# A decoder trunk's feed-forward stages: seven half-size block products per tile in place of eight, with the weight differences made on GpSimd

## The reference, cut to what matters

```
def swiglu(h, wg, wu, wd):
    return (jax.nn.silu(h @ wg) * (h @ wu)) @ wd
...
h = rmsnorm(x, ffn_norm_g[layer, 0])
x = x + 0.5 * swiglu(h, ffn_w_gate[layer, 0], ffn_w_up[layer, 0], ffn_w_down[layer, 0])
```

## Time and profile before

| | |
|---|---|
| median of three runs | 2102.38 us |
| span of the profiled execution | 2100.5 us |
| TensorE matmuls, busy | 2081.9 us (99%) |
| VectorE busy | 1205.3 us (57%) |
| ScalarE busy | 732.8 us (35%) |
| GpSimd busy | 107.2 us (5%) |
| chain that ended last | almost all TensorE |

### The profile page before, as it was taken

How to read it: one execution, slowest core, us unless ns; L and a number is a source line. 1 busy time by engine, 2 the same in 40 slices (tenths; PEclk the granted TensorE clock), 3 DMA queues, 4 the chain that set the end, 5 groups by cost and what they waited for, 6 DMA issues and landing times.

```text
span 2100.5 us, 30045 instructions
## 1 busy us (share of the span) xinstructions
PE 2081.9 (99%) x11183; PEld 1693.5 (81%) x11183; DVE 1205.3 (57%) x1925; ACT 732.8 (35%) x1029; POOL 107.2 (5%) x143
## 2 busy tenths in 40 slices
PE   8999999999999999999999999999999999999998
PEld 6888888788888888888888888888866688888887
DVE  6435445595777896444346544435679855444345
ACT  4212223453445442222124222222467742222223
POOL 0000000001000000000010000000026500000000
PEclk9999999999999999999999999999999999999999
DMA  6333433332253324454453333332310123333321
GB/s 174 100 100 91 112 88 93 92 92 72 61 141 96 86 81 120 103 117 104 110 114 103 100 100 90 100 100 76 110 46 1 41 71 100 92 99 91 100 87 64
DMA packets 357990, 195.17 MB, mean 93 GB/s; under 512 B 14891, under 2 KB 349878, under 8 KB 357894
## 3 DMA queue, kind: packets, MB, share of 16 engines
q1 hardware_dynamic: 355270, 184.21, 30.8%
q0 software_dynamic: 2624, 9.67, 2.9%
HBM read 191.07 MB, written 2.79 MB: 92 GB/s over the span
## 4 chain that ended last, share of the span: by engine, by line
PE 67%; DVE 4%; POOL 2%; issue 1%; ACT 0%; DVEq 0%; ACTq 0%; POOLq 0%
PE ps L1659 18%; PE ps L1657 18%; PE ps L1658 18%; PE ps L2276 1%; PE ps L2247 1%; POOL index_scores L490 1%; PE ps L2226 1%; PE ps L1989 1%; PE ps L1676 1%; PE ps L1991 1%; PE ps L1990 1%; PE ps L1677 1%; PE ps L1678 1%; POOL sq L487 1%; DVE w_lo L904 1%
## 5 line engine op out<-in xcount | busy, mean ns | idle before, releaser
L509 ACT ACTIVATE w_hi<-w_raw 128x1024 fp32r<-128x1024 f32 x351 | 371.7, 1060 | 1011.9 <-PE ps L1659 954.6
L1657 PE MATMUL ps<-h_hi,w_hi 128*128 128x512 f32 x1552 | 605.4, 390 | 0.0
L1658 PE MATMUL ps<-h_lo,w_hi 128*128 128x512 f32 x1552 | 603.8, 389 | 0.0
L1659 PE MATMUL ps<-h_hi,w_lo 128*128 128x512 f32 x1552 | 603.8, 389 | 0.0
L904 DVE TENSOR_TENSOR w_lo<-w_raw,w_hi 128x1024 fp32r<-128x1024 f32 x351 | 429.7, 1225 | 281.4 <-ACT w_hi L509 281.1
L1657 PEld LDWEIGHTS ps<-h_hi,w_hi 128*128 128x128 f32 x1552 | 291.4, 188 | 61.8 <-issue 1.7
L1659 PEld LDWEIGHTS ps<-h_hi,w_lo 128*128 128x128 f32 x1552 | 291.4, 188 | 60.6
L1658 PEld LDWEIGHTS ps<-h_lo,w_hi 128*128 128x128 f32 x1552 | 291.4, 188 | 60.0
L1657 PE MATMUL ps<-act_hi,w_hi 128*128 128x512 f32 x692 | 269.3, 389 | 0.0
L1659 PE MATMUL ps<-act_hi,w_lo 128*128 128x512 f32 x692 | 269.2, 389 | 0.0
L1658 PE MATMUL ps<-act_lo,w_hi 128*128 128x512 f32 x692 | 269.2, 389 | 0.0
(11 more groups left out here) (354 smaller groups left out, 2207.1 us busy)
## 6 DMA issues: line engine op xcount, KB each, us to landing
w_raw<-in_ffn_w_gate SPq DMA_DIRECT2D x88, 512.0 KB, 3.8
w_raw<-in_ffn_w_up SPq DMA_DIRECT2D x88, 512.0 KB, 3.8
w_raw<-in_ffn_w_down SPq DMA_DIRECT2D x64, 512.0 KB, 4.1
w_raw<-in_hy_w_in SPq DMA_DIRECT2D x44, 512.0 KB, 3.8
w_raw<-in_ffn_w_down SPq DMA_DIRECT2D x32, 384.0 KB, 3.5
w_raw<-in_hy_w_out SPq DMA_DIRECT2D x16, 512.0 KB, 3.8
acum_rows<-acum_scratch POOLq DMA_DIRECT2D x4, 1024.0 KB, 10.7
bias_rows<-line_scratch POOLq DMA_DIRECT2D x8, 512.0 KB, 6.8
```

The costliest lines, as they stand in the source:

```text
L509: act.activation(w_hi[:, s, :], w_raw[:, s, :], ACT.Copy).then_inc(hi_ready, 1)
L1657: pe.matmul(ps[:, bank, :], wh, rh[:, k, :], start=k == 0, stop=False)
L1658: pe.matmul(ps[:, bank, :], wh, rl[:, k, :], start=False, stop=False)
L1659: mm = pe.matmul(ps[:, bank, :], wl, rh[:, k, :], start=False, stop=k == nk - 1)
```

## The change

- The hidden tiles 4 to 21 of each stage (18 of 22; the first four stay as they were, `PLAIN`) are computed as a 2 x 2 block product with seven products instead of eight (`seven`). The 2 x 2 blocks of the weights are gate and up by the lower and upper half of the contraction; those of the input are the halves of the contraction by the halves of the tokens. Each product is 4 blocks x 3 matmuls of 256 columns, so a tile is 84 matmuls of 256 columns where it was 48 of 512.
- The products need sums and differences. Four blocks of the input are made once per stage by VectorE (`h_sums`, on `s_raw`, which ScalarE fills with eight scaled copies of `x`) and split into high and low parts (`s_high`, `s_low`). Per tile GpSimd makes four differences of weights of 128 x 512 (`weight_sums`): three into `mix_raw`, of which there is one, and one in place in the raw up unit. ScalarE rounds the 128 x 1536 of `mix_raw` (`t_high`), VectorE makes the low part (`t_low`). GpSimd starts a tile only when `t_low` of the tile before is done, and `load` now waits for its differences as well.
- The partial results are summed in PSUM where it can be done, and by small copies on ScalarE (`keep`, four of 128 x 256 per tile) and additions on VectorE (`gate_low`, `up_sums`, `gate_high`). TensorE waits for those copies between products (`kept`). The rounding of the activation moves from VectorE (L1042) to ScalarE (`act_high`).
- The down projection runs in phases of 4, 4, 4, 4 and 6 tiles. For the first four, two output columns are computed after each tile (`down_pack`: 24 matmuls of 512 columns), from one 512 KB unit that holds both. The last six tiles are done as eight down units at the stage's end.
- The loops over units are written out. The parameter transposes of `ffn0` come after its fourth tile. The bias rows of the attention are fetched after the last product of `ffn2` rather than during `ffn1`. Several semaphores are merged.

The core of the diff (of the two loops over `f` that follow `weight_sums`, the first is ScalarE's and the second VectorE's; `seven` and the last loop are TensorE's):

```
-PHASES = ((0, 8), (8, 8), (16, 6))
+HC = UC // 2
+PHASES = ((0, 4), (4, 4), (8, 4), (12, 4), (16, 6))
+PLAIN = 4
+BB, BA, BC = 0, 2, 6
...
+            def weight_sums(st, f):
+                u, k = gate_unit(st, f), (FT - PLAIN) * FFNS.index(st) + f - PLAIN
+                gate, up = w_raw[:, u % SLOTS, :], w_raw[:, (u + 1) % SLOTS, :]
+                pool.wait_ge(raw_landed[u % SLOTS], LAND[u])
+                pool.wait_ge(raw_landed[(u + 1) % SLOTS], LAND[u + 1])
+                if f > PLAIN:
+                    pool.wait_ge(t_lo_ready, k)
+                pool.tensor_tensor(mix_raw[:, 0:HC], up[:, 0:HC], gate[:, 0:HC], ALU.subtract).then_inc(t_made, 1)
+                pool.tensor_tensor(up[:, 0:HC], up[:, HC:UC], up[:, 0:HC], ALU.subtract).then_inc(t_made, 1)
+                pool.wait_ge(t_made, 4 * k + 1)
+                pool.tensor_tensor(mix_raw[:, HC:2 * HC], up[:, HC:UC], mix_raw[:, 0:HC], ALU.subtract).then_inc(t_made, 1)
+                pool.wait_ge(t_made, 4 * k + 3)
+                pool.tensor_tensor(mix_raw[:, 2 * HC:3 * HC], gate[:, HC:UC], mix_raw[:, HC:2 * HC], ALU.subtract).then_inc(t_made, 1)
...
+                for f in range(PLAIN, FT):
+                    nxt_unit = gate_unit(st, f) + 2
+                    if f == PLAIN:
+                        silu(f - 1)
+                    else:
+                        silu_half(f - 1, 1)
+                    if f == PLAIN:
+                        s_high(3)
+                    produce_hi(nxt_unit)
+                    act_high(f - 1)
+                    if f < FT - 1:
+                        t_high(f + 1)
+                    keep(f, 0)
+                    produce_hi(nxt_unit + 1)
...
+                for f in range(PLAIN, FT):
+                    nxt_unit = gate_unit(st, f) + 2
+                    added = 4 <= f - 1 < LAST + 4
+                    if f == PLAIN:
+                        scaled(f - 1)
+                    else:
+                        gate_high(f - 1)
+                    product(f - 1)
+                    if f == PLAIN:
+                        s_low(3)
+                    act_low(f - 1)
+                    if added:
+                        add_down(f - 1, 0)
+                    produce_lo(nxt_unit)
+                    if added:
+                        add_down(f - 1, 1)
+                    gate_low(f)
+                    produce_lo(nxt_unit + 1)
+                    if f < FT - 1:
+                        t_low(f + 1)
+                    if f < LAST + 4:
+                        produce_lo(nxt_unit + 2)
+                    up_sums(f)
...
+                def seven(f):
...
+                    product(b, gate, 0, *a11, True).then_inc(prod_done, 1)
...
+                    product(a, gate, HC, *a12, True).then_inc(unit_used, 1)
+                    pe.wait_ge(t_lo_ready, k + 1)
+                    pe.wait_ge(kept, 4 * k + 1)
...
+                    product(b, mixed, HC, *s2, False).then_inc(prod_done, 1)
...
+                    product(c, mixed, 0, *s1, True).then_inc(prod_done, 1)
+                    pe.wait_ge(lo_ready, u + 2)
+                    pe.wait_ge(kept, 4 * k + 2)
+                    product(b, up, 0, *s3, False).then_inc(prod_done, 1)
+                    pe.wait_ge(kept, 4 * k + 3)
...
+                    product(c, up, HC, *s4, False).then_inc(unit_used, 1)
+                    pe.wait_ge(kept, 4 * k + 4)
+                    product(b, mixed, 2 * HC, *a22, False).then_inc(prod_done, 1)
...
+                for f in range(PLAIN, FT):
+                    seven(f)
+                    if f < LAST + 4:
+                        down_pack(f)
```

More of the change, by code:

```diff
@@ L321, in columns @@
             def columns(n, w, c0, tiles, kt=KT):
-                with sp.Fori(0, tiles // 4) as i:
+                for i in range(tiles // 4):
                     for j in range(4):
-                        load(n + j, i, [(slot(n + j, kt), w[:, :, bass.ds(i * (4 * P) + (c0 + j * P), P)])])
+                        load(n + j, i, [(slot(n + j, kt), w[:, :, c0 + (4 * i + j) * P:c0 + (4 * i + j + 1) * P])])
                 return n + tiles
@@ L365, in _ @@
                     g_src, u_src, d_src = (kp(w[q // 2, q % 2]) for w in (wg, wu, wd))
[L366 to L370, removed]
+                    for f in range(FT):
+                        for j in range(2):
+                            if n + 2 * f + j > 1:
+                                load(gate_unit(st, f) + j, 0, [(slot(gate_unit(st, f) + j), (g_src, u_src)[j][:, :, f * P:(f + 1) * P])])
+                        if n == 0 and f == 1:
                             with nc.allow_non_contiguous_dma(reason="a few parameters, one number each"):
@@ new lines, in t_high @@
+                def t_high(f):
+                    k = kb + f - PLAIN
+                    act.wait_ge(t_made, 4 * (k + 1))
+                    if k >= 2:
+                        act.wait_ge(prod_done, 5 * (k - 1))
+                    act.activation(mix_hi[:, f % 2, :], mix_raw, ACT.Copy).then_inc(t_hi_ready, 1)
+                act.wait_ge(x_upd, XB[st])
+                for k in range(KT):
+                    act.activation(s_raw[:, k, :], x[:, k, :], ACT.Copy, scale=gains[:, GAIN[st] + k:GAIN[st] + k + 1]).then_inc(s_hi_ready, 1)
@@ new lines, in ffn @@
+                h_sums()
+                produce_lo(n + 4)
+                s_low(0)
+                scaled(0)
+                s_low(1)
+                product(0)
+                produce_lo(n + 5)
+                s_low(2)
+                act_low(0)
+                produce_lo(n + 6)
+                scaled(1)
+                product(1)
+                produce_lo(n + 7)
+                act_low(1)
+                t_low(PLAIN)
+                produce_lo(n + 8)
+                scaled(2)
@@ new lines, in ffn, with product @@
+                n, q = UB[st], FFNS.index(st)
+                fb, gb, kb = FT * q, PLAIN * q, (FT - PLAIN) * q
+                xc = XB[st] + NDOWN
+                def product(dst, w_at, c0, rh, rl, start):
+                    for k in range(4):
+                        wh, wl = (w[:, c0 + k * P:c0 + (k + 1) * P] for w in w_at)
+                        pe.matmul(dst, wh, rh[:, k, :], start=start and k == 0, stop=False, skip_group_check=True)
+                        pe.matmul(dst, wh, rl[:, k, :], start=False, stop=False, skip_group_check=True)
+                        mm = pe.matmul(dst, wl, rh[:, k, :], start=False, stop=k == 3, skip_group_check=True)
+                    return mm
@@ L1826, in half_sums @@
+                for m in range(2, KT if nxt != "final" else KT - 2):
+                    down(m, range(LAST_N))
+                if nxt == "final":
+                    last_halves(n, LAST_N, xc)
             def half_sums(g):
```

552 lines of the change are left out of this document (355 added, 197 removed).

## The result

The changed kernel takes 2090.14 us (median of four runs, 2087.45 to 2091.61) beside 2103.25 us of the kernel before (four runs here): a ratio of 0.9937, with a 95% interval of 0.9923 to 0.995. It is faster by 13.1 us where 28 were forecast.

What follows compares the result with a forecast made beforehand. TensorE's matmul stream was taken to bound the feed-forward stages. -57.6 + 6.4 + 20 + 3.6 = -27.6 took the profiled 2100.5 to 2072.9, medians 1.9 above: 2075 us; own range 2058 to 2088, full range 2050 to 2125.

Steps and rivals of the forecast that it cites:

- moved and costed at nothing: Bias rows fetched from `ffn2`'s last product: 54 us at most plus under 20 of additions, at least 15 us of cover.
- a wait in the scores: Sign of a wrong forecast: TensorE waiting in the scores for the bias rows; any excess shows there one to one.
- The saving of 57.6: Tiles 4 to 21: 84 matmuls at 120.0 ns, 10.08 us instead of 10.88; 72 x 0.80 = 57.6 us.
- The loop: From one tile's second product to the next's third, through VectorE, load, GpSimd and ScalarE: 15.4 us of 15.52 allowed.
- The third product: Sign: TensorE waits almost all on ScalarE's copy there, about 5 us at tile 4, 1 at tile 21, under 0.3 between.
- (a): Rival: the port costs nothing on the path, only 1.8 + 0.9 us per stage remain, 2055.6 us; chance 0.2.
- the 353 us named: Sign of a right forecast: feed-forward stages of about 353 us, against 360.58 measured before.
- The steady turn: Tiles 5 to 20, four stages: 0.1 us lost per turn in 64 turns, 6.4 us, with 1.9 for the port.
- Tile 4: Start of each stage: third product waits 5.3 us, 1.8 without port turns; four stages, 20 us.
- Tile 21: End of each stage: no pack before it, the copy waits behind `act_high(20)`; 0.9 x 4 = 3.6 us.
- rival (c): TensorE's clock falls in the pauses, 1.2 GHz for one tile per stage, 40 us: 2115 us; chance 0.03.

Runs made afterwards that it cites:

- experiment 2: Kernel before, with only the eight bias-row fetches held until `ffn2`'s last up unit is used, no block products: 2123.35 us, ratio 1.0097.
- experiment 4: Changed kernel with the eight bias-row fetches issued behind units 1, 3, 5, 7, 9, 11, 12 and 13 of `ffn2`'s tail: 2066.78 us, ratio 0.9826.
- experiment 6: Changed kernel with GpSimd's first weight difference made twice per tile, with a wait between: 2147.28 us, ratio 1.0213.
- experiment 8: Changed kernel; in `ffn0` alone, tile 0's gate, product and low part ahead of the four input sums and `s_low`: 2091.09 us, ratio 0.9947.
- experiment 9: Changed kernel; in `ffn0`, gates, products and splits of tiles 0 and 1 ahead of the four input sums: 2089.25 us, ratio 0.9935.
- experiment 1: Changed kernel with the bias-row fetches issued one by one behind every second unit of the tail, mask built first: 2085.9 us, ratio 0.9918.
- experiment 3: Changed kernel with the bias-row fetches behind units 1, 3, 4, 6, 7, 9, 10 and 12 of the tail: 2079.65 us, ratio 0.9893.
- experiment 5: Changed kernel with ScalarE's copy `keep(f, 0)` ahead of `t_high(f+1)` at tiles 4 to 20: 2085.13 us, ratio 0.9915.
- experiment 12: Changed kernel with fetches behind units 1, 3, 5, 7, 9, 11, 12, 13, first product's copy before `t_high`, and before `act_high(20)` at tile 21: 2060.46 us, ratio 0.9797.

## Why the prediction was right or wrong

**What failed is the step "moved and costed at nothing".** It priced the bias rows by their 6.8 us of landing and asked only when GpSimd is wanted next; by that there were 15 us of cover, and a shortfall would have shown in the scores. Two things were wrong in it. The 6.8 was measured with a wait of seven units between one fetch and the next, and the diff takes that wait away: a duration read in one arrangement was used in another. And I asked only for the consumer of the rows, while the weight loads share the DMA engines with them and TensorE has no more than four slots of weights ahead. The price was 23 us (25.5 over the ideal in `ffn2`, less 1.5 and 0.6 for tiles 4 and 21), and experiments 2 and 4 give 20.0 and 23.4 for it from both sides. That is more than the 12.7 us by which the spans miss the forecast; the other terms together came out better than forecast. A sign of it was named, a wait in the scores, and it was the wrong place to look: the weights starved from 1471 to 1493 us, before the stage was over.

**What held.** The saving of 57.6: the step of 120.0 ns stands in the timelines of the changed kernel (905.04, 905.40, 905.76: three matmuls each), the plain mixer stage did not move (224.61 against 224.64), and nearly all of what was given back has a place. The Trainium skill (TensorE: Matmul & The Clock Gate, Back-to-back issue gap) has a formula for the gap of an isolated matmul that gives 109.2 ns; the stream of the changed kernel is above it again, at 120.0. The loop is where it was said to be, and experiment 6 shows it. The third product is where TensorE waits, at tile 4 and tile 21, by the engines named. Of the rivals, (a) describes the steady tiles best, though the port is not free: with the fetches paced the kernel takes 2066.8, and with tiles 4 and 21 mended 2060.5, beside its 2055.6. `ffn1` and the last stage are shorter than the 353 us named (350.4 and 348.0), `ffn2` is longer (371.7).

**What was mis-sized.**
- *The steady turn*: 6.4 us forecast, 0 measured. The chain's front part was right (from the second product's end at 907.92 to GpSimd's next start at 914.04 it is 6.12 us, by the prediction 6.3; 6.97 in the turn shown, with its slow load) and so was its end (1.79 against 1.9). GpSimd's four operations took 5.96 us where 7.25 were assumed: 0.6 for the port, not 1.9. That leaves 15.52 - 6.12 - 5.96 - 1.79 = 1.65 us of slack instead of 0.1. The turns for the port are taken, but it is mostly VectorE that waits: its products take 1468 ns in the mean, not 692.
- *Tile 4*: 20 us forecast, 8.2 measured (2.3, 2.7, 1.5 and 1.7). My queue for VectorE was added up with every step in series, and with the port's turns in full.
- *Tile 21*: 3.6 forecast, 2.6 measured.
- *The clock* (rival (c), 0.03): it does fall, in `ffn0` and in the starved end of `ffn2`, and was no rival but a surcharge. In `ffn0` 4.3 us of the 10.7 are left after the pauses of 3.40, 2.32 and 0.6; the granted clock of the three windows accounts for about 3.3 of them (19 x 0.08, 11.5 x 0.01 and 8.5 x 0.19), and for the last 1.0 no place was found.
- *`ffn0`'s start*: not in the sum at all. I read the start of `ffn1` for all four stages; `ffn0` has no mixer ahead of it, and its scaled copies of `x` come late. 3.4 us, and experiments 8 and 9 could only move them.

By terms, then: -57.6, +8.2 for tile 4, +2.6 for tile 21, +3.4 for the pause of `ffn0` and +4.3 for what is left there, most of it the clock, +23.3 for the fetches, and 0.9 for the rest: -14.9, the difference of the two spans.

## What to carry to other kernels

When a diff moves transfers, price them by who shares the queues and the DMA engines at their new place, and look for the wait that used to space them: the duration in the old profile was measured under it. Issued within 4.5 us, these cost 20 to 23; over 62 us, nothing that can be seen. And before spending an idle engine's time on a loop, measure how far the loop is from its period by adding one more operation; here that told that the loop had room for less than one more.

## What the runs showed of the hardware that was not expected

- *A burst of eight fetches of a skewed pattern, 4 MB, and one plain fetch of 512 KB holds up others more than its bytes.* A weight load among them took 41.18 us and one issue of SyncE 23.86. With the fetches spaced by one or two units the DMA share was about the same (1.17 and 0.99, beside 1.07 and 1.02), the engines moved 160 and 205 GB/s instead of 127 and 138, and a fetch landed in 7.9 us instead of 24.0. How the queues divide the engines was not tried.
- *Who pays for the shared port.* In the turn shown, VectorE's operation begun at 900.76 ends 0.55 us after GpSimd's, which ends at 901.93: it took 1.72 us, not 0.69. The Trainium skill (SBUF — State Buffer, SBUF: two separate sides) has the port pair as a lock for a whole instruction, and the trace agrees. What it does to the sum depends on which of the two has the longer instructions and the slack: GpSimd's last operation there ends 1.15 us after VectorE's second (905.33 and 904.18), the same step as in the earlier trace rows. GpSimd's four lost 0.6 us in all, and VectorE's product alone takes 1468 ns in the mean instead of 692.
- *The clock after a pause is not told by its length.* In the changed kernel's trace the pause of 2.32 us in `ffn0` was followed by a granted clock of 0.81, so partly at the 1.2 GHz level, and those of 2.73, 1.54 and 1.66 us in the later stages by 1.00. But the stage does not decide it either. The kernels of experiments 1, 4, 8 and 9 have the same code at the start of `ffn1`, and there pauses of 2.79, 2.33, 2.68 and 2.26 us were followed by 0.83, 0.81, 0.80 and 0.80, while the 2.77 us of experiment 3 were followed by 1.00. The windows behind that pause in the changed kernel and in experiment 1:

```profile
830.00:838.50 8.50, 8.43 (x66) 8.24 (x66) 6.88 (x9) 3.74 (x8) 1.15 (x1) 1.00 0.61 180
829.85:838.35 8.50, 8.50 (x60) 8.50 (x61) 6.49 (x8) 3.25 (x6) 1.45 (x2) 0.83 0.61 181
```

  At these lengths the same place in the same code comes out both ways, and it is worth about 1 us: `ffn1` takes 351.67 and 351.34 us in experiments 1 and 4, 350.42 and 350.48 in the changed kernel and in experiment 3. With the pause in `ffn0` cut to 0.94 and 0.98 us (experiments 5 and 12) the window behind it had 1.00.
